# Between two layers of a streamed network: another order of weight chunks on TensorE, and low halves moved from GpSimd to VectorE

## The chip, the cores and the metric

The kernel runs on one core of a Trainium2 chip. The metric is the device time of one execution in microseconds (us). The engines are called TensorE (PE in the profile), VectorE (DVE), ScalarE (ACT), GpSimd (POOL) and SyncE (SP, which here only issues transfers).

## The reference

A sequence of 256 rows of 1024 numbers goes through a first block (a mixer, a cross attention, a mixture of experts, a final norm) and then through two layers of a second block. What matters here is the seam between layer 0 and layer 1 of that second block:

```python
def _rms_norm(x, g):
    xf = x.astype(jnp.float32)
    y = xf * lax.rsqrt(jnp.mean(xf * xf, axis=-1, keepdims=True) + NORM_EPS)
    return (y * g.astype(jnp.float32)).astype(x.dtype)

for i in range(DEPTH_2):                      # two layers
    h = _rms_norm(x, norm_mix_pre[i])
    proj = h @ w_in[i]                        # its first columns here: v and g_out
    ...
    y = (jax.nn.gelu(a, approximate=False) * b) @ ffn_w_down[i]
    x = x + _rms_norm(y, norm_ffn_post[i])    # the seam: the next layer starts with this x
```

## The kernel before

**Chunks of weights.** All weights are streamed from memory in units of 1 MB into a ring of seven slots (`RING`); one unit is two chunks of 128 x 1024. Products are made in three passes, for which every operand is split into a high and a low half: ScalarE writes the high half of a chunk (`WH<-RING`, `hi_half`), then VectorE or GpSimd subtracts it from the chunk and writes the low half (`RINGL<-RING,WH`, `lo_half`). Chunks listed in `LOW_ON_POOL` get their low half on GpSimd, all others on VectorE. There are six buffers for high halves (`NH = 6`): the high half of chunk c waits until TensorE has used up chunk c - 6.

**Chunks of the seam.** Layer l begins with the chunks v0 to v3 (values) and g0 to g3 (output gate), then the pool chunks. The 256 rows of the sequence are two tiles of 128, t = 0 and 1. `stream_tile(c0, j, t)` multiplies chunk j of a group of four into tile t alone: six matmuls of 128x512 (two slices k of the contraction, three passes each). `stream_rows` does the same chunk for both tiles, twelve matmuls. A chunk counts as used up when its tile 1 is done. v_j and g_j need the slices k = 2j and 2j + 1 of the activation.

**The raw activation.** So that the next layer can begin before the norm of its input is known, its first eight chunks are multiplied with the raw activation times the gain (`rh_mix`, `rl_mix`), and the scale of the norm is put in later. `raw_turn` transposes tile t of X with eight small matmuls (`P<-CONS,X`), in two halves of four; ScalarE turns each half into four high slices (`rh_mix`, `norm_hi`), VectorE into four low slices (`rl_mix`, `norm_lo`). `norm_turn` does it again later with the true scale (`P<-DIAG,X`, result in `HA` and `LA`), for all the chunks from pool on.

**The residual.** The end of layer 0 gives four banks, tile 0 in P4 and P5, tile 1 in P6 and P7. For each tile ScalarE sums the squares (`JNK`), VectorE multiplies by the gain (`YB`), forms the mean, ScalarE the root (`SM<-SM`), and VectorE adds the result to X (`X<-YB,SM,X`, twice 128x512 for each tile). `raw_turn` of tile 1 waits for the two X of tile 1.

Order of work is written out by hand in each engine's program: `tensor_layer` for TensorE, `scalar_layer` for ScalarE, `vector_layer` for VectorE, `gpsimd_layer` for GpSimd. Each engine works through its list in order, and waits on semaphores. `hi_until(end)` and `lo_until(end)` do all high or low halves up to chunk `end` that are not yet done. GpSimd's part for the seam is the `tail` of `gpsimd_layer(0)`, three low halves, and the `low` of `gpsimd_layer(1)`, two more:

```python
    tail = [c for c in sorted(LOW_ON_POOL) if c >= chunk_of(1, "v") and c < chunk_of(1, "g")] if l == 0 else []
    ...
    for c in low:
        if c >= chunk_of(l, "g"):
            lo_half(e, m, s, c)
```

Of the kernel before, what the change touches and what calls it, by code (L numbers as in the profile page):

```python
# [23 lines left out]
GROUPS = 16  # L24
# [129 lines left out]
class Port:  # L154
# [70 lines left out]
    def overflow(self, most):  # L225
# [4 lines left out]
        else:  # L230
            name = str(self.engine.engine).split(".")[-1]
            self.engine.br_cond(self.count < most + 1, f"fits_{name}", f"over_{name}").branch_hint(self.seen)
            with self.engine.bass.body(f"over_{name}", valid_engines=[self.engine.engine]):
# [22 lines left out]

LOW_ON_POOL = {1, 3} | {B2 + l * L_CHUNKS + L_AT[n] + i for l, n, i in
                        ((0, "v", 0), (0, "v", 3), (0, "g", 0), (0, "g", 2),
                         (1, "v", 0), (1, "v", 1), (1, "v", 3), (1, "g", 0), (1, "g", 2),
                         (0, "ffn", 12), (1, "ffn", 12))}  # L260


# [420 lines left out]
def rstd_columns(m, t, base):  # L683
    return (m.SM[:, base + 8 + 4 * t + i:base + 9 + 4 * t + i] for i in range(4))
# [21 lines left out]
def rstd_root(e, m, s, tag, t, base=200):  # L706

    rstd_log(e, m, s, tag, t, base)
    rstd_exp(e, m, s, tag, t, base)
# [14 lines left out]
def rstd_end(e, m, s, tag, t, base=200):  # L724

    rstd_step(e, m, s, tag, t, base)
    rstd_last(e, m, s, tag, t, base)
# [11 lines left out]
def norm_turn(e, m, s, tag, x, t):  # L739

    e.wait_ge(*s.diag[tag, t])
    for i in range(2):
        b = 4 + 2 * t + i
        for q in range(4):
            k = 4 * i + q
            for sig, event in m.free[b]:
                e.wait_ge(*sig[event])
            p = e.matmul(m.P[b][:, q * 128:(q + 1) * 128], x[:, t, k * 128:(k + 1) * 128], m.DIAG[:, t, :],
                         start=True, stop=True)
        p.then_inc(*s.turned.up(tag, t, i))  # L750
        m.free[b] = [(s.norm_lo, (tag, t, 4 * i + 3))]


def norm_hi(e, m, s, tag, hi, gain, t, i):

    e.wait_ge(*s.turned[tag, t, i])
    for q in range(4):
        k = 4 * i + q
        e.activation(hi[:, k, t * 128:(t + 1) * 128], m.P[4 + 2 * t + i][:, q * 128:(q + 1) * 128], ACT.Copy,
                     scale=m.par(gain, k)).then_inc(*s.norm_hi.up(tag, t, k))  # L760
# [65 lines left out]
def stream_rows(e, m, s, chunks, j, a, freed, pairs=(0, 1, 2, 3)):  # L826

    end = len(chunks) - 1
    if j == 0:
        for t in range(2):  # L830
            m.next_bank((chunks[0], t), True)
    c = chunks[j]
    hi, lo = m.hi(c), m.lo(c)
    e.wait_ge(*s.hi[c])
    for i in range(2):
        k = 2 * pairs[j] + i
        w = slice(i * 512, (i + 1) * 512)
        for t in range(2):
            b = m.bank[chunks[0], t]
            ta = slice(t * 128, (t + 1) * 128)  # L840
            first, last = j == 0 and i == 0, j == end and i == 1
            sig, event = a.hi_mark(k, t)
            e.wait_ge(*sig[event])
            if first:
                for sig, event in m.free[b]:
                    e.wait_ge(*sig[event])
            e.matmul(m.P[b][:, :], a.hi[:, k, ta], hi[:, w], start=first, stop=False)
            e.wait_ge(*s.lo_of(c)[c])
            e.matmul(m.P[b][:, :], a.hi[:, k, ta], lo[:, w], start=False, stop=False)
            sig, event = a.lo_mark(k, t)  # L850
            e.wait_ge(*sig[event])
            p = e.matmul(m.P[b][:, :], a.lo[:, k, ta], hi[:, w], start=False, stop=last)
            if last and t == 0:
                p.then_inc(*s.stream.up("t0", c))
                m.held.discard(b)
                m.free[b] = [freed(0)]
    p.then_inc(*s.stream.up(c))
    if j == end:
        m.held.discard(b)
        m.free[b] = [freed(1)]  # L860


def stream_tile(e, m, s, c0, j, t, a, freed, pairs=(0, 1, 2, 3)):

    if j == 0:
        m.next_bank((c0, t))
    b = m.bank[c0, t]
    p = rows_part(e, m, s, c0 + j, j, t, b, a, pairs)
    if t == 1:
        p.then_inc(*s.stream.up(c0 + j))  # L870
    elif j == 3:
        p.then_inc(*s.stream.up("t0", c0 + j))
    if j == 3:
        m.free[b] = [freed]
# [1940 lines left out]
def chunk_of(l, name, i=0):  # L2815
    return B2 + l * L_CHUNKS + L_AT[name] + i
# [76 lines left out]
def raw_turn(e, m, s, tag, t, marks):  # L2893

    for i in range(2):
        b = 4 + 2 * t + i
        sig, event = marks[i]
        e.wait_ge(*sig[event])
        for sig, event in m.free[b]:
            e.wait_ge(*sig[event])  # L2900
        for q in range(4):
            k = 4 * i + q
            p = e.transpose(m.P[b][:, q * 128:(q + 1) * 128], m.X[:, t, k * 128:(k + 1) * 128], m.con("ident"))
        p.then_inc(*s.turned.up("raw " + tag, t, i))
        m.free[b] = [(s.norm_lo, ("raw " + tag, t, 4 * i + 3))]
# [12 lines left out]
def tensor_layer(e, m, s, l):  # L2918
    mix, ffn = f"mix{l}", f"ffn{l}"
    chunk = lambda name, i=0: chunk_of(l, name, i)  # L2920
# [1 line left out]
    a = normed(s, mix, m.HA, m.LA)  # L2922


    for t in range(2):
        for j in range(4):
            if (t, j) == (0, 3 if l else 1):
                if l:
                    raw_turn(e, m, s, "mix1", 1, [(s.resid, (0, 1, 1, n)) for n in range(2)])
                else:  # L2930
                    raw_turn(e, m, s, "mix0", 1, [(s.drain, ("moe", GROUPS - 1, 1, n)) for n in range(2)])
            stream_tile(e, m, s, chunk("v"), j, t, raw, (s.evac, ("vv", l, t)))
    step = lambda j: stream_rows(e, m, s, range(chunk("g"), chunk("g") + 4), j, raw, lambda t: (s.evac, ("go", l, t)))
    step(0)
    norm_turn(e, m, s, mix, m.X, 0)
    step(1)
    norm_turn(e, m, s, mix, m.X, 1)
    step(2)
    step(3)
    for i in range(4):  # L2940
        stream_t(e, m, s, chunk("pool", i), a, (s.evac, ("px", l, i)))
    q = lambda h: stream_t(e, m, s, head_chunk(l, 0, h), a, (s.evac, ("q", l, h)))
# [313 lines left out]
def scalar_raw(e, m, s, tag, gain, t):  # L3256
    hi = m.RAW[tag][0]
    norm_hi(e, m, s, "raw " + tag, hi, gain, t, 0)
    norm_hi(e, m, s, "raw " + tag, hi, gain, t, 1)
# [7 lines left out]
def scalar_layer(e, m, s, l):  # L3267
# [202 lines left out]
            hi_until(e, m, s, down_chunk(l, i - 2) + 5)  # L3470
    hi_until(e, m, s, chunk("ffn", 66))
    e.preload_act_table_set("natural_log_exp_and_others")
    e.wait_ge(*s.product["down", l, 0, 0])
    scalar_post(e, m, s, l, 1, 0, 0, m.P[4])
    e.wait_ge(*s.product["down", l, 0, 1])
    scalar_post(e, m, s, l, 1, 0, 1, m.P[5])
    rstd_root(e, m, s, f"post{l}1", 0, base=224)
    if l == 0:
        hi_until(e, m, s, chunk_of(1, "v", 2))
    e.wait_ge(*s.product["down", l, 1, 0])  # L3480
    scalar_post(e, m, s, l, 1, 1, 0, m.P[6])
    e.wait_ge(*s.stream[down_chunk(l, 21)])
    scalar_post(e, m, s, l, 1, 1, 1, m.P[7])
    if l == 0:
        scalar_raw(e, m, s, "mix1", "mix_pre1", 0)
        hi_until(e, m, s, chunk_of(1, "g"))
    rstd_root(e, m, s, f"post{l}1", 1, base=224)


def scalar_beside(e, m, s, l, n):  # L3490
# [67 lines left out]
def scalar_post(e, m, s, l, w, t, n, bank):  # L3558
    square(e, m, s, bank[:, :], m.SM[:, 224 + 2 * t + n:225 + 2 * t + n], (1.0 / D) ** 0.5, f"post{l}{w}", t, n)
# [83 lines left out]
def vector_raw(e, m, s, tag, gain, t):  # L3643
    hi, lo = m.RAW[tag]
    norm_lo(e, m, s, "raw " + tag, hi, lo, gain, t, 0)
    norm_lo(e, m, s, "raw " + tag, hi, lo, gain, t, 1)
# [7 lines left out]
def vector_post(e, m, s, l, w, t, n, bank):  # L3654

    e.wait_ge(*s.square[f"post{l}{w}", t, n])
    e.wait_ge(*s.vec["gain", l, w])
    e.tensor_tensor(m.YB[:, t, n * 512:(n + 1) * 512], bank[:, :], m.GB[:, n * 512:(n + 1) * 512],
                    ALU.mult).then_inc(*s.drain.up("post", l, w, t, n))


def vector_post_tile(e, m, s, l, w, t, bank):

    tag = f"post{l}{w}"
    e.wait_ge(*s.square[tag, t, 1])
    rstd_mean(e, m, s, tag, t, base=224)
    vector_post(e, m, s, l, w, t, 1, bank)
    rstd_end(e, m, s, tag, t, base=224)
    mean, y, a, r = rstd_columns(m, t, 224)
    e.wait_ge(*s.rstd[tag, t])  # L3670
    for n in range(2):
        x = m.X[:, t, n * 512:(n + 1) * 512]
        e.wait_ge(*s.drain["post", l, w, t, n])
        e.scalar_tensor_tensor(x, m.YB[:, t, n * 512:(n + 1) * 512], r, x, ALU.mult, ALU.add).then_inc(*s.resid.up(l, w, t, n))
# [7 lines left out]
def vector_layer(e, m, s, l):  # L3682
# [124 lines left out]
    for i in range(22):  # L3807
# [21 lines left out]
        if 1 < i < 20:  # L3829
            lo_until(e, m, s, down_chunk(l, i - 2) + 5)  # L3830
    lo_until(e, m, s, chunk("ffn", 66))
    vector_post(e, m, s, l, 1, 0, 0, m.P[4])
    vector_post_tile(e, m, s, l, 1, 0, m.P[5])
    if l == 0:
        lo_until(e, m, s, chunk_of(1, "v", 2))
    vector_post(e, m, s, l, 1, 1, 0, m.P[6])
    if l == 0:
        vector_raw(e, m, s, "mix1", "mix_pre1", 0)
        lo_until(e, m, s, chunk_of(1, "g"))
    vector_post_tile(e, m, s, l, 1, 1, m.P[7])  # L3840


def vector_final_norm(e, m, s):
# [362 lines left out]
```

## Time and profile before

| | |
|---|---|
| median of three runs | 1645.8 us (1643.89 to 1646.1) |
| the profiled execution | 1644.13 us, its span 1642.3 us |
| TensorE busy | 1592.4 us, 97% |
| VectorE busy | 937.3 us, 57% |
| ScalarE busy | 729.3 us, 44% |
| GpSimd busy | 90.2 us, 5% |
| mean granted TensorE clock | 0.994 of full |
| transfers | 243 GB/s over the span |

The span runs from the first to the last instruction of the profiled execution. Times inside the trace are us from its start. The seam between the layers lies at 1178 to 1213 us.

### The profile page before, as it was taken

How to read it: one execution, taken by the hardware profiler on the slowest of the kernel's cores; microseconds unless marked ns; L12 is line 12 of the kernel's file. 1: busy time of each engine (PE TensorE's matmuls, PEld its weight loads, DVE VectorE, ACT ScalarE, POOL GpSimd, SP SyncE). 2: the span in 40 equal slices, each digit the busy share in tenths (PEclk: the TensorE clock that was granted, in tenths of full speed). 3: DMA queues.
4: the chain of work that ended last, by engine and by line, in shares of the span. 5: the costliest groups of instructions: out<-in, count | busy, mean ns of one | idle time of the engine just before them, and what ended most of it. 6: DMA issues, size and time to landing. Idle time of an engine off the chain costs nothing.

```text
span 1642.3 us, 22882 instructions
## 1 busy us (share of the span) xinstructions
PE 1592.4 (97%) x9321; PEld 1200.3 (73%) x9321; DVE 937.3 (57%) x1595; ACT 729.3 (44%) x1385; POOL 90.2 (5%) x81
## 2 busy tenths in 40 slices
PE   7999999999999999989999999999899999999998
PEld 6987885444333434339997889999799978889997
DVE  5967655232332332247675567766767855677665
ACT  6755542110110111047663357555566633575554
POOL 1010000000000000014001000000230010000000
PEclk9999999999999999999999999999999999999999
DMA  9433578999999999994444445555443444545550
GB/s 358 179 129 132 195 292 314 389 378 423 424 424 400 424 423 424 423 377 178 143 169 155 175 171 189 180 182 187 154 177 132 180 154 166 180 167 183 190 192 27
DMA packets 57414, 399.83 MB, mean 243 GB/s; under 512 B 6612, under 2 KB 7029, under 8 KB 9946
## 3 DMA queue, kind: packets, MB, share of 16 engines
q1 hardware_dynamic: 57306, 398.34, 63.0%
q8 instruction: 74, 1.21, 0.3%
q14 instruction: 34, 0.28, 0.0%
HBM read 397.26 MB, written 1.05 MB: 243 GB/s over the span
## 4 chain that ended last, share of the span: by engine, by line
PE 82%; DMA 12%; DVE 3%; ACT 2%; POOL 0%; issue 0%; SPq 0%; DVEq 0%; POOLq 0%
PE P L171 80%; DMA RING<-in_ws_dram 8%; PE P L174 2%; DMA ew<-in_ws_dram 1%; DMA W<-in_hw_dram 1%; DMA ez<-in_ws_dram 1%; DVE RINGL L183 1%; DVE X L189 0%; POOL GV L183 0%; ACT WH L177 0%; DVE SM L189 0%; DVE rl_mix L189 0%; ACT JNK L177 0%; DVE YB L183 0%; SPq L216 0%
## 5 line engine op out<-in xcount | busy, mean ns | idle before, releaser
L183 DVE TENSOR_TENSOR RINGL<-RING,WH 128x1024 fp32r<-128x1024 f32 x338 | 418.9, 1272 | 130.2 <-ACT WH L177 129.0
L177 ACT ACTIVATE WH<-RING 128x1024 fp32r<-128x1024 f32 x351 | 358.1, 1055 | 53.0 <-PE P L171 50.8
L171 PE MATMUL P<-HA,WH 128*128 128x256 f32 x1208 | 345.3, 286 | 0.0
L171 PE MATMUL P<-LA,WH 128*128 128x256 f32 x1208 | 340.5, 282 | 0.0
L171 PE MATMUL P<-HA,RINGL 128*128 128x256 f32 x1208 | 340.5, 282 | 0.0
L171 PEld LDWEIGHTS P<-HA,WH 128*128 128x128 f32 x1208 | 227.9, 189 | 5.8 <-issue 3.0
L171 PEld LDWEIGHTS P<-HA,RINGL 128*128 128x128 f32 x1208 | 228.4, 189 | 2.1
L171 PEld LDWEIGHTS P<-LA,WH 128*128 128x128 f32 x1208 | 228.8, 189 | 0.0
L171 PE MATMUL P<-RING,XT 128*64 128x512 f32 x632 | 143.9, 595 | 8.2 <-DMA RING<-in_ws_dram 8.1
L171 PEld LDWEIGHTS P<-RING,XT 128*64 128x64 f32 x632 | 44.1, 137 | 103.4 <-issue 78.2
L171 PE MATMUL P<-WH,HA 128*128 128x512 f32 x272 | 110.5, 406 | 1.3 <-ACT VN L177 1.3
L183 DVE TENSOR_TENSOR GS<-P,GS 128x512 f32<-128x512 f32 x16 | 11.1, 692 | 173.1 <-PE P L171 173.1
L171 PE MATMUL P<-RINGL,HA 128*128 128x512 f32 x272 | 107.4, 395 | 1.8 <-POOL RINGL L183 1.8
L171 PE MATMUL P<-WH,LA 128*128 128x512 f32 x272 | 106.9, 393 | 0.0
L189 DVE SCALAR_TENSOR_TENSOR YSL<-P,SM,YSH 128x512 fp32r<-128x512 f32 x32 | 22.6, 747 | 127.2 <-ACT YSH L177 127.2
L177 ACT ACTIVATE YSH<-P,SM 128x512 fp32r<-128x512 f32 x32 | 20.3, 684 | 142.1 <-PE P L171 142.1
L177 ACT ACTIVATE HT<-P 128x512 f32<-128x512 f32 x16 | 9.6, 598 | 153.7 <-PE P L174 153.7
L189 DVE SCALAR_TENSOR_TENSOR CVT<-QPC,PARS,CVT 128x256 f32<-128x256 f32 x104 | 53.5, 515 | 36.4 <-ACT CVT L177 34.2
L171 PE MATMUL P<-WH,FL 128*128 128x512 f32 x176 | 69.8, 397 | 0.0
L171 PE MATMUL P<-RINGL,FH 128*128 128x512 f32 x176 | 69.4, 395 | 0.0
L171 PE MATMUL P<-WH,FH 128*128 128x512 f32 x176 | 69.3, 394 | 0.0
L177 ACT ACTIVATE QPC<-P 128x256 f32<-128x256 f32 x68 | 26.0, 382 | 86.2 <-PE P L171 86.2
(404 smaller groups left out, 2676.8 us busy)
## 6 DMA issues: line engine op xcount, KB each, us to landing
RING<-in_ws_dram SPq DMA_DIRECT2D x288, 1024.0 KB, 5.0
ew<-in_ws_dram SPq DMA_DIRECT2D x47, 1024.0 KB, 21.5
ez<-in_ws_dram SPq DMA_DIRECT2D x16, 1024.0 KB, 20.0
ek<-in_ws_dram SPq DMA_DIRECT2D x6, 1024.0 KB, 10.9
ef<-in_ws_dram SPq DMA_DIRECT2D x4, 1024.0 KB, 10.7
eha<-in_ws_dram SPq DMA_DIRECT2D x2, 1024.0 KB, 5.1
ela<-in_ws_dram SPq DMA_DIRECT2D x2, 1024.0 KB, 6.8
TAB<-in_dft_dram SPq DMA_DIRECT2D x2, 1024.0 KB, 5.6
```

The lines of the kernel that those rows point to most:

```text
L171: return self.engine.matmul(*a, **k) if self.engine else self
L174: return self.engine.transpose(*a) if self.engine else self
L177: return self.engine.activation(*a, **k) if self.engine else self
L183: return self.engine.tensor_tensor(*a) if self.engine else self
L189: return self.engine.scalar_tensor_tensor(*a) if self.engine else self
```

## The change

The change touches the seam between layer 0 and layer 1 only. It has three parts. The chunks v0, v1, v3, g0 and g2 of layer 1 get their low half on VectorE, no longer on GpSimd. On ScalarE and VectorE the halves of the first chunks move ahead: v0 to v2 (ScalarE) and v0, v1 (VectorE) come before the squares and gains of the last product, and the residual sum of tile 1 (`vector_post_sum`) comes after the low halves of v3 and g0. On TensorE tile 0 goes through v0 to v3 and g0 before the raw turn of tile 1, and through g1 right behind it; then tile 1 does the same six chunks. g2 and g3 stay with the norm turns, now tile by tile.

```diff
--- before.py
+++ after.py
@@ -256,7 +256,6 @@
 
 LOW_ON_POOL = {1, 3} | {B2 + l * L_CHUNKS + L_AT[n] + i for l, n, i in
                         ((0, "v", 0), (0, "v", 3), (0, "g", 0), (0, "g", 2),
-                         (1, "v", 0), (1, "v", 1), (1, "v", 3), (1, "g", 0), (1, "g", 2),
                          (0, "ffn", 12), (1, "ffn", 12))}
 
 
@@ -2922,21 +2921,38 @@
     a = normed(s, mix, m.HA, m.LA)
 
 
-    for t in range(2):
+    v = lambda j, t: stream_tile(e, m, s, chunk("v"), j, t, raw, (s.evac, ("vv", l, t)))
+    go = lambda j, t: stream_tile(e, m, s, chunk("g"), j, t, raw, (s.evac, ("go", l, t)))
+    if l == 0:
+        for t in range(2):
+            for j in range(4):
+                if (t, j) == (0, 1):
+                    raw_turn(e, m, s, "mix0", 1, [(s.drain, ("moe", GROUPS - 1, 1, n)) for n in range(2)])
+                v(j, t)
+        step = lambda j: stream_rows(e, m, s, range(chunk("g"), chunk("g") + 4), j, raw, lambda t: (s.evac, ("go", l, t)))
+        step(0)
+        norm_turn(e, m, s, mix, m.X, 0)
+        step(1)
+        norm_turn(e, m, s, mix, m.X, 1)
+        step(2)
+        step(3)
+    else:
+
         for j in range(4):
-            if (t, j) == (0, 3 if l else 1):
-                if l:
-                    raw_turn(e, m, s, "mix1", 1, [(s.resid, (0, 1, 1, n)) for n in range(2)])
-                else:
-                    raw_turn(e, m, s, "mix0", 1, [(s.drain, ("moe", GROUPS - 1, 1, n)) for n in range(2)])
-            stream_tile(e, m, s, chunk("v"), j, t, raw, (s.evac, ("vv", l, t)))
-    step = lambda j: stream_rows(e, m, s, range(chunk("g"), chunk("g") + 4), j, raw, lambda t: (s.evac, ("go", l, t)))
-    step(0)
-    norm_turn(e, m, s, mix, m.X, 0)
-    step(1)
-    norm_turn(e, m, s, mix, m.X, 1)
-    step(2)
-    step(3)
+            v(j, 0)
+        go(0, 0)
+        raw_turn(e, m, s, "mix1", 1, [(s.resid, (0, 1, 1, n)) for n in range(2)])
+        go(1, 0)
+        for j in range(4):
+            v(j, 1)
+        go(0, 1)
+        go(1, 1)
+        norm_turn(e, m, s, mix, m.X, 0)
+        go(2, 0)
+        go(2, 1)
+        norm_turn(e, m, s, mix, m.X, 1)
+        go(3, 0)
+        go(3, 1)
     for i in range(4):
         stream_t(e, m, s, chunk("pool", i), a, (s.evac, ("px", l, i)))
     q = lambda h: stream_t(e, m, s, head_chunk(l, 0, h), a, (s.evac, ("q", l, h)))
@@ -3470,21 +3486,25 @@
             hi_until(e, m, s, down_chunk(l, i - 2) + 5)
     hi_until(e, m, s, chunk("ffn", 66))
     e.preload_act_table_set("natural_log_exp_and_others")
+    if l == 0:
+        hi_until(e, m, s, chunk_of(1, "v", 3))
     e.wait_ge(*s.product["down", l, 0, 0])
     scalar_post(e, m, s, l, 1, 0, 0, m.P[4])
     e.wait_ge(*s.product["down", l, 0, 1])
     scalar_post(e, m, s, l, 1, 0, 1, m.P[5])
     rstd_root(e, m, s, f"post{l}1", 0, base=224)
     if l == 0:
-        hi_until(e, m, s, chunk_of(1, "v", 2))
+        hi_until(e, m, s, chunk_of(1, "g"))
     e.wait_ge(*s.product["down", l, 1, 0])
     scalar_post(e, m, s, l, 1, 1, 0, m.P[6])
     e.wait_ge(*s.stream[down_chunk(l, 21)])
     scalar_post(e, m, s, l, 1, 1, 1, m.P[7])
+    hi = m.RAW["mix1"][0]
     if l == 0:
-        scalar_raw(e, m, s, "mix1", "mix_pre1", 0)
-        hi_until(e, m, s, chunk_of(1, "g"))
+        norm_hi(e, m, s, "raw mix1", hi, "mix_pre1", 0, 0)
     rstd_root(e, m, s, f"post{l}1", 1, base=224)
+    if l == 0:
+        norm_hi(e, m, s, "raw mix1", hi, "mix_pre1", 0, 1)
 
 
 def scalar_beside(e, m, s, l, n):
@@ -3661,13 +3681,21 @@
 
 def vector_post_tile(e, m, s, l, w, t, bank):
 
+    vector_post_end(e, m, s, l, w, t, bank)
+    vector_post_sum(e, m, s, l, w, t)
+
+
+def vector_post_end(e, m, s, l, w, t, bank):
     tag = f"post{l}{w}"
     e.wait_ge(*s.square[tag, t, 1])
     rstd_mean(e, m, s, tag, t, base=224)
     vector_post(e, m, s, l, w, t, 1, bank)
     rstd_end(e, m, s, tag, t, base=224)
+
+
+def vector_post_sum(e, m, s, l, w, t):
     mean, y, a, r = rstd_columns(m, t, 224)
-    e.wait_ge(*s.rstd[tag, t])
+    e.wait_ge(*s.rstd[f"post{l}{w}", t])
     for n in range(2):
         x = m.X[:, t, n * 512:(n + 1) * 512]
         e.wait_ge(*s.drain["post", l, w, t, n])
@@ -3829,15 +3857,21 @@
         if 1 < i < 20:
             lo_until(e, m, s, down_chunk(l, i - 2) + 5)
     lo_until(e, m, s, chunk("ffn", 66))
+    if l == 0:
+        lo_until(e, m, s, chunk_of(1, "v", 2))
     vector_post(e, m, s, l, 1, 0, 0, m.P[4])
     vector_post_tile(e, m, s, l, 1, 0, m.P[5])
     if l == 0:
-        lo_until(e, m, s, chunk_of(1, "v", 2))
+        lo_until(e, m, s, chunk_of(1, "v", 3))
     vector_post(e, m, s, l, 1, 1, 0, m.P[6])
+    hi, lo = m.RAW["mix1"]
     if l == 0:
-        vector_raw(e, m, s, "mix1", "mix_pre1", 0)
-        lo_until(e, m, s, chunk_of(1, "g"))
-    vector_post_tile(e, m, s, l, 1, 1, m.P[7])
+        norm_lo(e, m, s, "raw mix1", hi, lo, "mix_pre1", 0, 0)
+    vector_post_end(e, m, s, l, 1, 1, m.P[7])
+    if l == 0:
+        norm_lo(e, m, s, "raw mix1", hi, lo, "mix_pre1", 0, 1)
+        lo_until(e, m, s, chunk_of(1, "g", 1))
+    vector_post_sum(e, m, s, l, 1, 1)
 
 
 def vector_final_norm(e, m, s):
```

On VectorE, at the seam, before the change (the rows from the sum of tile 0 into X; `rl_mix` are the low slices of the raw activation, `RINGL` low halves of weights, `SM` the small columns of the norm):

```order
L189 SCALAR_TENSOR_TENSOR X<-YB,SM,X 128x512 x2
L183 TENSOR_TENSOR YB<-P,GB 128x512
L189 SCALAR_TENSOR_TENSOR rl_mix_188<-P,PARS,rh_mix_187 128x128 x8
L183 TENSOR_TENSOR RINGL<-RING,WH 128x1024
L186 TENSOR_SCALAR SM<-SM 128x1
L183 TENSOR_TENSOR YB<-P,GB 128x512
L189 SCALAR_TENSOR_TENSOR SM<-SM 128x1 x2
L189 SCALAR_TENSOR_TENSOR X<-YB,SM,X 128x512 x2
L183 TENSOR_TENSOR RINGL<-RING,WH 128x1024
```

The same place of VectorE with the change:

```order
L189 SCALAR_TENSOR_TENSOR X<-YB,SM,X 128x512 x2
L183 TENSOR_TENSOR RINGL<-RING,WH 128x1024
L183 TENSOR_TENSOR YB<-P,GB 128x512
L189 SCALAR_TENSOR_TENSOR rl_mix_188<-P,PARS,rh_mix_187 128x128 x4
L186 TENSOR_SCALAR SM<-SM 128x1
L183 TENSOR_TENSOR YB<-P,GB 128x512
L189 SCALAR_TENSOR_TENSOR SM<-SM 128x1 x2
L189 SCALAR_TENSOR_TENSOR rl_mix_188<-P,PARS,rh_mix_187 128x128 x4
L183 TENSOR_TENSOR RINGL<-RING,WH 128x1024 x2
L189 SCALAR_TENSOR_TENSOR X<-YB,SM,X 128x512 x2
L183 TENSOR_TENSOR RINGL<-RING,WH 128x1024
```

Between the two sums into X there is now one low half ahead of the gain (v2) and two behind the low slices (v3, g0), where there was one (v2); the norm's small steps moved between the two halves of the low slices.

On ScalarE, at the seam, before the change (`JNK` are the squares, `SM` the roots, `WH` high halves of weights, `rh_mix` high slices of the raw activation):

```order
L180 ACT_TABLE_LOAD
L177 ACTIVATE JNK,SM<-P 128x512 x2
L177 ACTIVATE SM<-SM 128x1 x2
L177 ACTIVATE WH<-RING 128x1024 x2
L177 ACTIVATE JNK,SM<-P 128x512 x2
L177 ACTIVATE rh_mix_187<-P,PARS 128x128 x8
L177 ACTIVATE WH<-RING 128x1024 x2
L177 ACTIVATE SM<-SM 128x1 x2
L177 ACTIVATE WH<-RING 128x1024 x2
```

The same place of ScalarE with the change:

```order
L180 ACT_TABLE_LOAD
L177 ACTIVATE WH<-RING 128x1024 x3
L177 ACTIVATE JNK,SM<-P 128x512 x2
L177 ACTIVATE SM<-SM 128x1 x2
L177 ACTIVATE WH<-RING 128x1024
L177 ACTIVATE JNK,SM<-P 128x512 x2
L177 ACTIVATE rh_mix_187<-P,PARS 128x128 x4
L177 ACTIVATE SM<-SM 128x1 x2
L177 ACTIVATE rh_mix_187<-P,PARS 128x128 x4
L177 ACTIVATE WH<-RING 128x1024 x2
```

Three high halves now stand ahead of the first squares, and the roots of tile 1 between the two halves of the high slices.

## Rows read from the trace of the kernel before

**Rows 1.** Page, part 1: engine, busy us, share of the span, instructions.

```profile
PE 1592.4 (97%) x9321; PEld 1200.3 (73%) x9321; DVE 937.3 (57%) x1595; ACT 729.3 (44%) x1385; POOL 90.2 (5%) x81
```

**Rows 2.** TensorE's waits, 1176 to 1642 us: in total, times, longest.

```profile
PE P L174 <- DVE X L189: 4.4, 3, 1.8
PE P L171 <- DVE RINGL L183: 0.3, 1, 0.3
```

**Rows 3.** Timeline of TensorE: start, us, engine, line, out<-in, count [idle before].

```profile
1177.95 0.60 PE L174 MATMUL P<-CONS,X 128*128 128x128 f32 x4
1179.48 0.66 PE L174 MATMUL P<-CONS,X 128*128 128x128 f32 x4 [0.93 <-DVE X L189]
...
1181.37 0.40 PE L171 MATMUL P<-WH,rh_mix 128*128 128x512 f32 x1
...
1182.99 0.40 PE L171 MATMUL P<-WH,rh_mix 128*128 128x512 f32 x1
1183.66 0.50 PE L171 MATMUL P<-RINGL,rh_mix 128*128 128x512 f32 x1 [0.27 <-DVE RINGL L183]
...
1184.69 0.39 PE L171 MATMUL P<-WH,rl_mix 128*128 128x512 f32 x1
1186.91 1.11 PE L174 MATMUL P<-CONS,X 128*128 128x128 f32 x4 [1.83 <-DVE X L189]
1189.66 1.12 PE L174 MATMUL P<-CONS,X 128*128 128x128 f32 x4 [1.64 <-DVE X L189]
1190.43 0.78 PE L171 MATMUL P<-WH,rh_mix 128*128 128x512 f32 x1
...
1193.82 0.40 PE L171 MATMUL P<-WH,rl_mix 128*128 128x512 f32 x1
...
1201.61 1.95 PE L171 MATMUL P<-DIAG,X 128*128 128x128 f32 x16
...
1213.42 0.28 PE L171 MATMUL P<-HA,WH 128*128 128x256 f32 x1
```

**Rows 4.** Timeline of VectorE between the layers.

```profile
1174.01 0.69 DVE L183 TENSOR_TENSOR YB<-P,GB 128x512 f32<-128x512 f32 x1 [3.81 <-ACT JNK L177]
...
1175.88 3.55 DVE L189 SCALAR_TENSOR_TENSOR X<-YB,SM,X 128x512 f32<-128x512 f32 x2
...
1179.95 1.11 DVE L189 SCALAR_TENSOR_TENSOR rl_mix<-P,PARS,rh_mix 128x128 fp32r<-128x128 f32 x4
...
1182.40 1.21 DVE L183 TENSOR_TENSOR RINGL<-RING,WH 128x1024 fp32r<-128x1024 f32 x1
...
1186.10 3.50 DVE L189 SCALAR_TENSOR_TENSOR X<-YB,SM,X 128x512 f32<-128x512 f32 x2
```

**Rows 5.** Timeline of GpSimd between the layers.

```profile
1176.42 5.26 POOL L183 TENSOR_TENSOR RINGL<-RING,WH 128x1024 fp32r<-128x1024 f32 x2 [153.25 <-ACT WH L177]
...
1186.18 2.87 POOL L183 TENSOR_TENSOR RINGL<-RING,WH 128x1024 fp32r<-128x1024 f32 x1
```

**Rows 6.** Timeline of VectorE, end of layer 1, where GpSimd is idle.

```profile
1634.22 1.41 DVE L189 SCALAR_TENSOR_TENSOR X<-YB,SM,X 128x512 f32<-128x512 f32 x2
```

**Rows 7.** Timeline of ScalarE between the layers.

```profile
1168.96 1.28 ACT L180 ACT_TABLE_LOAD   x1
...
1178.74 1.14 ACT L177 ACTIVATE rh_mix<-P,PARS 128x128 fp32r<-128x128 f32 x4
...
1183.77 0.44 ACT L177 ACTIVATE SM<-SM 128x1 f32<-128x1 f32 x2 [0.56 <-DVE SM L186]
```

**Rows 8.** Windows: us, busy of each engine, granted clock, DMA share, GB/s.

```profile
508.00:516.00 8.00, 8.00 (x24) 2.39 (x26) 0.53 (x1) 0.00 (x0) 0.00 (x0) 0.60 1.01 424
723.00:729.00 6.00, 3.55 (x18) 2.29 (x18) 5.45 (x11) 6.00 (x14) 3.38 (x2) 1.00 1.01 422
1176.00:1190.00 14.00, 9.33 (x42) 6.38 (x41) 13.64 (x19) 10.18 (x24) 11.03 (x7) 0.88 0.35 120
1186.80:1193.50 6.70, 4.95 (x15) 3.95 (x16) 6.32 (x12) 3.83 (x13) 2.25 (x1) 0.50 0.00 0
```

## The prediction

> **What bounds the kernel now.** The page's first part says that TensorE is busy for 1592.4 of 1642.3 us, while VectorE and ScalarE are at 57% and 44% [rows 1]: only what TensorE loses can be won. The view of TensorE's waits from the end of layer 0 to the end of the program shows where that is. There are four waits in all, 4.7 us together: three for a sum into X ahead of transposes, one for a low half [rows 2]. The last of them is at 1189.66 [rows 3]; in the 450 us of layer 1 behind it TensorE waits for nothing. A microsecond that TensorE gains at the seam therefore stays gained, as long as the engines that feed it move up as well, and everything on them there hangs on TensorE's progress or on the same X.
>
> The timeline of TensorE through the seam [rows 3] gives the pace. From 1193.82 to 1201.61 it issues 34 matmuls of 128x512 without a gap: 7.79 / 34 = 0.229 us each, so one chunk for one tile (six matmuls) is 1.37 us. Against that pace the seam loses time at four places behind 1181.37, where the second chunk begins:
> - at v2 (1182.99 to 1183.66 where one step of 0.23 would do): 0.44 us, for its low half; v1 waits similarly for about 0.1;
> - from 1184.92 (1184.69 + 0.23) to 1186.91: 1.99 us, for the first X of tile 1;
> - in the raw turn of tile 1: it begins at 1186.91 and the next matmul stands at 1190.43, 3.52 us. The turn of tile 0 gives four transposes in 0.60; four more at that pace bring a turn to about 1.05. Lost: 2.47 us, the wait for the second X (1.64) and a slow clock;
> - from 1190.43 to 1193.82 eight matmuls take 3.39 instead of 1.83 us: 1.56 lost. The windows show why: the granted clock is 0.50 of full, the 1.2 GHz level, in 1186.8 to 1193.5, right behind the idle time of 1.83 us [rows 8].
>
> That is 0.54 + 1.99 + 2.47 + 1.56 = 6.6 us in which TensorE stands or crawls, and it is the most that a change of the seam can win behind 1181.37.
>
> **Why X is late.** VectorE's two sums into X of tile 1 take 3.50 us, and those of tile 0 take 3.55 [rows 4]. The same two instructions at the end of layer 1 take 1.41 [rows 6]. The difference is what runs on GpSimd: its low halves occupy 1176.42 to 1181.68 and 1186.18 to 1189.05 [rows 5], and each pair of sums lies across the beginning of one. VectorE's own low half, 1.21 us, and its low slices out of PSUM, 1.11 us for four [rows 4], have the length that they have elsewhere.
>
> **The change part by part.**
>
> *GpSimd.* Five low halves leave it. Each returns as one VectorE instruction of 1.21 us (about 1.15 from start to start). The two pairs of sums fall from 3.5 to 1.41, a gain of 2.1 us each.
>
> *v0 and v1 early.* VectorE is idle for 3.81 us before 1174.01 [rows 4], so both low halves, 2.4 us, lie in a hole and cost nothing; without the hole they would delay the gain by 2.4 us. On ScalarE three high halves of about 1.0 us stand behind the table load, which ends at 1170.24 (1168.96 + 1.28 [rows 7]). The third needs a buffer that TensorE frees at about 1172.4, so it ends at 1173.6 and the first squares start about 0.3 us late. VectorE absorbs that: the sum of tile 0 ends at 1177.6 instead of 1179.4.
>
> *Raw turn of tile 0.* It no longer waits in its middle (the 0.93 of 1179.48 [rows 3]). That gives nothing by itself: ScalarE starts its high slices at 1178.74 [rows 7], behind its squares, VectorE starts the low slices at 1179.95 as before, and TensorE's third matmul of v0 needs the first of them. So 1181.37 stays where it is, and I count from there.
>
> *Walk behind 1181.37.* TensorE does v1 until 1182.7. On VectorE the first four low slices end at 1181.1; mean, gain and small steps follow, with ScalarE's roots at 1181.3 to 1181.7 (it started 0.24 behind the mean before too, 1183.77 [rows 7]). Then come ScalarE's second four high slices, to 1182.8, and VectorE's low ones, 1182.8 to 1183.9. v2 needs the first of these at 1183.2: just in time; it ends at 1184.1. v3 needs its low half, which VectorE makes behind the slices, 1183.9 to 1185.1. TensorE waits 0.75 us here: this is the new wait, and the only one of any size. v3 ends at 1186.25, g0, whose low half is ready at 1186.2, at 1187.6. The sums of tile 1 follow at 1186.15 and end at 1187.55, so the turn at 1187.6 finds both. It ends at 1188.7, just when the low half of g1 is ready (1188.7). g1 ends at 1190.1. By then the slices of tile 1 have begun (ScalarE from about 1188.35, VectorE from 1189.5), and the next six chunks run at full pace for 8.25 us, to 1198.3.
>
> *Norm turns and behind.* At 1198.3 the first norm turn starts; before it started at 1201.61 [rows 3] with two chunk tiles less done. Its scale is ready at about 1195. Two norm turns (1.95 busy [rows 3], of which the next matmuls cover 0.25, so 1.70 each) and the four tiles of g2 and g3 (5.5 us) put the first pool chunk at about 1207.4, against 1213.42 [rows 3]. g2's low half on VectorE ends near 1197.7 and is needed at 1200: hidden, as is g0's extra 1.15 in the walk. The six high buffers hold exactly v0 to g1; g2's needs v0's, which tile 1 frees at 1191.5. SyncE's fetches hang on the same marks and come slightly earlier.
>
> **The sum.** The losses of 6.6 us, less the new wait of 0.75 (0.8 with small ones): 5.8 us. The walk gives 6.0. I take 5.9. The profiled execution took 1644.13 us (span 1642.3 and 1.8 around it); it would take 1638.2. It lies 1.7 under the median of 1645.8, so the median goes to **1639.9**, a change of 0.36%. About 0.2% (3.3 us) is what a measurement of this kernel can tell from no change.
>
> **A rule that speaks against it.** VectorE is busy for 13.64 of the 14 us from 1176 to 1190 [rows 8], and the change gives it more to do there. The Trainium skill, Perfetto Trace Analysis, section Optimizing Scalar/DVE Operations, says that when VectorE is saturated, handing work to ScalarE or even GpSimd may make sense, and adds that the two share a read port, so that it might not help between them. Going by its first half the change would win next to nothing, as the second rival works out; by its second half, the sum above. The rows lean to the second half: the pairs of sums lose 2.1 us each beside GpSimd.
>
> **The rivals.**
> 1. *The clock falls anyway.* The forecast has TensorE idle for 0.6 us at 1179.7 and 0.75 at 1184.4. Against a fall: at the first layer's seam it was busy for only 3.55 of 6 us and the clock stayed at 1.00 (723 to 729 [rows 8]). For it: at this seam it fell. A half rate stretch of 6.7 us like the one before, now under full load, costs 3.35, and the gain is 2.5: 1643.3. Chance 13%.
> 2. *VectorE becomes the bound.* If GpSimd was not what stretched the sums, they keep 3.5 us, and with two more halves (2.3 us) ahead of them the second X comes at 1189.6 + 2.3 = 1191.9. Behind it lie a piece of the turn, g1 and ten more tiles (15.1 us) and two norm turns: pool at 1210.9, and with the clock fallen by 1.6 more at 1212.5. Gain about 1: 1644.9. Rows 6 speak against it. Chance 7%.
> 3. *Half way.* One wait more of 1 to 2.5 us, for instance the pair of sums not wholly freed, or a high half late behind the roots: gain 4, 1641.8. Chance 10%.
> 4. *Slower.* One mechanism: the clock falls at 1184.4 and stays low under full load. Each microsecond at the 1.2 GHz level costs half of one, so the gain is gone at 11.8 us of it, and at 19 us the kernel is 3.6 us slower: 1649.4. The stretch around 508 to 516 shows 0.60 over 8 us, about 6.4 us at the low level [rows 8], and the one of this seam 6.7; neither is near. Chance 4%.
>
> **How the numbers follow.** Forecast 66%, rivals 13, 7, 10 and 4%. The forecast has its own spread of about 1.5 us (all 6.6 won, or a wait of 1.5 more, and the spread of medians): 1637.8 to 1641.6. To leave out no more than 2 in 10 the range goes up to rival 1: 1637.5 to 1643.6. Faster by over 0.2% (under 1642.5): nearly all of the forecast, two thirds of rival 3, a fourth of rival 1, together 0.75. Slower: 0.04. The rest is 0.21.
>
> **What the changed profile would show.** Right: no GpSimd low halves at the seam; pairs of sums at 1.4 us; one TensorE wait for RINGL of about 0.75 at v3 and none for X; clock 1.00 through 1178 to 1213; from 1181.4 to the first pool chunk 26 us instead of 32.05; no waits behind it. Wrong would be sums still at 3.5, a clock of 0.50 somewhere behind 1179, a wait of over a microsecond at v2 or at the first norm turn, or TensorE waiting in layer 1 where it did not before.

## The result

| | before | changed |
|---|---|---|
| median of six runs | 1644.08 us (1642.81 to 1646.1) | 1637.42 us (1636.43 to 1637.92) |
| profiled execution | 1644.13 us, span 1642.3 | 1636.43 us, span 1634.6 |
| the seam (see below) | 46.70 us | 40.47 us |

The ratio is 0.9962, with a 95% interval of 0.9953 to 0.9972: 6.2 us faster (4.6 to 7.7), where 5.9 were forecast. The median of the kernel before came out at 1644.08 over six runs, 1.7 us under the 1645.8 of three runs that the forecast started from. So the absolute number, 1637.42, lies 2.5 us under the forecast 1639.9 and just under the low end of its range (1637.5), most of it by that starting level and not by the change.

The first rows of the page of the changed kernel answer to [rows 1]: GpSimd is busy for 14 us less, TensorE for 4.9 us less. Of these 4.9 us, 2.7 are the slow clock at the seam, as the windows below show; the rest had arisen ahead of it, where the two programs are the same.

```profile
span 1634.6 us, 22882 instructions
...
PE 1587.5 (97%) x9321; PEld 1197.4 (73%) x9321; DVE 937.0 (57%) x1600; ACT 729.0 (45%) x1385; POOL 76.1 (5%) x76
```

TensorE's waits from the end of layer 0 to the end of the program answer to [rows 2]. The three waits for a sum into X are gone; 1.1 us are left, and none lies behind the seam.

```profile
PE P L171 <- DVE RINGL L183: 0.5, 1, 0.5
PE P L171 <- DVE rl_mix L189: 0.4, 1, 0.4
PE P L171 <- issue: 0.2, 1, 0.2
```

The timeline of TensorE through the seam answers to [rows 3]:

```profile
1165.26 0.28 PE L171 MATMUL P<-LA,WH 128*128 128x256 f32 x1
...
1178.85 0.50 PE L171 MATMUL P<-WH,rl_mix 128*128 128x512 f32 x1 [0.41 <-DVE rl_mix L189]
...
1179.87 0.39 PE L171 MATMUL P<-WH,rh_mix 128*128 128x512 f32 x1
...
1182.66 0.40 PE L171 MATMUL P<-WH,rh_mix 128*128 128x512 f32 x1
1183.54 0.50 PE L171 MATMUL P<-RINGL,rh_mix 128*128 128x512 f32 x1 [0.48 <-DVE RINGL L183]
...
1186.17 1.04 PE L174 MATMUL P<-CONS,X 128*128 128x128 f32 x8
1186.96 0.47 PE L171 MATMUL P<-WH,rh_mix 128*128 128x512 f32 x1
...
1196.66 1.95 PE L171 MATMUL P<-DIAG,X 128*128 128x128 f32 x16
...
1205.73 0.28 PE L171 MATMUL P<-HA,WH 128*128 128x256 f32 x1
```

"The seam" is from here on the time from the last matmul of the last up chunk (`P<-LA,WH`, at 1165.26 here, at 1166.72 before) to the first of the first pool chunk (1205.73 here, 1213.42 before). It is a better measure of a change of this size than one execution's span: the spans differ by 7.7 us, of which 1.46 had arisen before this stretch, where the two programs are the same. Behind it both take 428.9 us. The windows of exactly this stretch, in the kernel before and in the changed one (us, then busy time of TensorE, of its weight loads, of VectorE, ScalarE and GpSimd, then granted clock, DMA share, GB/s):

```profile
1166.72:1213.42 46.70, 42.03 (x196) 33.79 (x194) 32.37 (x65) 30.44 (x74) 13.43 (x8) 0.93 0.40 144
```

```profile
1165.26:1205.73 40.47, 39.37 (x196) 32.21 (x195) 30.00 (x70) 30.05 (x74) 0.50 (x3) 1.00 0.50 182
```

The same 196 matmuls are busy for 2.66 us less, and TensorE is idle for 1.10 us instead of 4.67: 6.23 together.

The timeline of VectorE answers to [rows 4], and the windows to [rows 8]:

```profile
1169.88 2.36 DVE L183 TENSOR_TENSOR RINGL<-RING,WH 128x1024 fp32r<-128x1024 f32 x2 [1.15 <-ACT WH L177]
1172.80 0.69 DVE L183 TENSOR_TENSOR YB<-P,GB 128x512 f32<-128x512 f32 x1 [0.56 <-ACT JNK L177]
...
1174.57 1.42 DVE L189 SCALAR_TENSOR_TENSOR X<-YB,SM,X 128x512 f32<-128x512 f32 x2
1175.90 1.22 DVE L183 TENSOR_TENSOR RINGL<-RING,WH 128x1024 fp32r<-128x1024 f32 x1
...
1178.44 1.13 DVE L189 SCALAR_TENSOR_TENSOR rl_mix<-P,PARS,rh_mix 128x128 fp32r<-128x128 f32 x4 [0.72 <-ACT rh_mix L177]
...
1181.22 1.13 DVE L189 SCALAR_TENSOR_TENSOR rl_mix<-P,PARS,rh_mix 128x128 fp32r<-128x128 f32 x4 [0.62 <-ACT rh_mix L177]
1182.27 2.35 DVE L183 TENSOR_TENSOR RINGL<-RING,WH 128x1024 fp32r<-128x1024 f32 x2
1184.54 1.41 DVE L189 SCALAR_TENSOR_TENSOR X<-YB,SM,X 128x512 f32<-128x512 f32 x2
```

```profile
1176.00:1190.00 14.00, 12.90 (x62) 9.93 (x61) 11.72 (x27) 8.93 (x28) 0.00 (x0) 1.00 0.28 102
1190.00:1205.00 15.00, 15.00 (x83) 12.96 (x82) 9.98 (x29) 11.90 (x33) 0.00 (x0) 1.00 0.74 268
```

Both pairs of sums take 1.4 us. Two low halves fill the hole behind 1169.9. The clock is at 1.00 throughout. VectorE, which has more instructions than before, is busy for 11.72 of these 14 us instead of 13.64.

### The profile page after: what moved, and what is told of

Same layout as the page of the kernel before. It is cut to its first block, busy times and chain, and to the rows that moved or that the text cites. A ratio compares the mean times of both kernels' runs of the same rounds, so it can differ in the third digit from the quotient of the medians.

```text
span 1634.6 us, 22882 instructions
## 1 busy us (share of the span) xinstructions
PE 1587.5 (97%) x9321; PEld 1197.4 (73%) x9321; DVE 937.0 (57%) x1600; ACT 729.0 (45%) x1385; POOL 76.1 (5%) x76
## 3 DMA queue, kind: packets, MB, share of 16 engines
q8 instruction: 74, 1.21, 0.3%
HBM read 397.26 MB, written 1.05 MB: 244 GB/s over the span
## 4 chain that ended last, share of the span: by engine, by line
PE 82%; DMA 13%; DVE 3%; ACT 2%; issue 0%; SPq 0%; DVEq 0%
PE P L171 80%; DMA RING<-in_ws_dram 8%; DMA ew<-in_ws_dram 2%; PE P L174 2%; DMA ez<-in_ws_dram 1%; DMA W<-in_hw_dram 1%; DVE RINGL L183 1%; ACT WH L177 0%; DVE rl_mix L189 0%; ACT JNK L177 0%; DVE SM L189 0%; ACT SM L177 0%; ACT L180 0%; DVE HS L189 0%; ACT rh_mix L177 0%
## 5 line engine op out<-in xcount | busy, mean ns | idle before, releaser
L183 DVE TENSOR_TENSOR RINGL<-RING,WH 128x1024 fp32r<-128x1024 f32 x343 | 424.4, 1270 | 128.0 <-ACT WH L177 127.0
```

The source lines that it names most:

```text
L183: return self.engine.tensor_tensor(*a) if self.engine else self
```

## The experiments

Each kernel was compared with runs of the kernel before on the same chip (medians 1644.1, 1644.2 and 1644.05 us, and a single run of 1644.55). The seam is read from each run's own profile. "Run-ahead" is TensorE's new order (tile 0 goes on through v3 and g0 before the raw turn of tile 1, and through g1 behind it), "early split" the new order of ScalarE and VectorE (the halves of the first chunks ahead of the squares, gains and sums).

| kernel | median us | ratio, interval | seam us |
|---|---|---|---|
| before (three executions profiled) | | | 46.70, 46.13, 47.49 |
| changed (two) | 1637.4 | 0.9962 (0.9953 to 0.9972) | 40.47, 40.48 |
| GpSimd part alone | 1639.6 | 0.9975 (0.9964 to 0.9987) | 42.55 |
| changed, low halves kept on GpSimd | 1638.1 | 0.9966 (0.9954 to 0.9978) | 42.78 |
| changed, TensorE's old order | 1641.1 | 0.9984 (0.9975 to 0.9993) | 44.29 |
| changed, without the early split | 1638.8 | 0.9967 (0.9953 to 0.9980) | 42.28 |
| changed, g2 alone on GpSimd | 1638.2 | 0.9962 (0.9947 to 0.9977) | 40.47 |
| layer 0's seam off GpSimd too | 1636.4 | 0.9951 (0.9937 to 0.9964) | 40.50 |
| the same, v3's low half earlier | 1635.0 | 0.9945 (0.9931 to 0.9959) | 40.15 |
| the same, low slices first at layer 0 | 1635.4 | 0.9947 (0.9933 to 0.9960) | 40.14 |

**The GpSimd part alone.** The kernel before, with

```diff
-                         (1, "v", 0), (1, "v", 1), (1, "v", 3), (1, "g", 0), (1, "g", 2),
```

> The kernel before with one part of the change: the five chunks of layer 1 get their low half on VectorE; every order stays. Theory (GpSimd's low halves stretch the sums into X, and the new order hides the halves that come back): the sums of tile 1 take 1.4 us instead of 3.5, but v0, v1 and v3 now stand ahead of them on VectorE (3.5 us), so the first one ends only about 2 us earlier and the first matmuls of v0 start late; gain 2 to 4 us of the 6.2. Rival A (the neighbourhood of GpSimd is all there is to it): gain about 6 us. Rival B (the order is all): no gain, or slower by up to 1 us.

Measured: 4.1 us by the ratio, 4.15 by the seam, just above the 2 to 4 us that were expected. VectorE's timeline shows four low halves between the sums, and both pairs at 1.4 us. TensorE's shows what is left: one wait for the first sum of tile 1, and then a whole turn in one piece.

```profile
1175.18 1.41 DVE L189 SCALAR_TENSOR_TENSOR X<-YB,SM,X 128x512 f32<-128x512 f32 x2
1176.52 2.35 DVE L183 TENSOR_TENSOR RINGL<-RING,WH 128x1024 fp32r<-128x1024 f32 x2
...
1181.46 2.34 DVE L183 TENSOR_TENSOR RINGL<-RING,WH 128x1024 fp32r<-128x1024 f32 x2
...
1184.88 1.42 DVE L189 SCALAR_TENSOR_TENSOR X<-YB,SM,X 128x512 f32<-128x512 f32 x2
```

```profile
1185.68 1.32 PE L174 MATMUL P<-CONS,X 128*128 128x128 f32 x8 [1.54 <-DVE X L189]
1186.76 0.48 PE L171 MATMUL P<-WH,rh_mix 128*128 128x512 f32 x1
```

**The new orders, with GpSimd kept.** The changed kernel with that line put back.

> The changed kernel with the five low halves put back on GpSimd; the new orders stay. Theory: VectorE has 5.8 us less to do but its sums meet GpSimd again: the pair of tile 0 meets v3's low half and ends near 3 us, everything behind it is about 1 us late, g0's low half (2.5 us on GpSimd) lands about 1.5 us late and meets the sums of tile 1. Loss 1 to 2.5 us against the changed kernel, so a gain of 4 to 5 against before. Rival (VectorE, 94% busy before at the seam, is the bound and the move to it costs): as fast as the changed kernel or up to 1 us faster.

The seam is 2.3 us longer than in the changed kernel although VectorE has five instructions less, and 3.9 shorter than before. VectorE's timeline shows why: both pairs of sums are back at over 3.5 us, each beside one low half of GpSimd.

```profile
1174.34 3.53 DVE L189 SCALAR_TENSOR_TENSOR X<-YB,SM,X 128x512 f32<-128x512 f32 x2
...
1183.34 3.58 DVE L189 SCALAR_TENSOR_TENSOR X<-YB,SM,X 128x512 f32<-128x512 f32 x2
```

```profile
1174.50 2.82 POOL L183 TENSOR_TENSOR RINGL<-RING,WH 128x1024 fp32r<-128x1024 f32 x1 [0.41 <-ACT WH L177]
...
1183.28 2.41 POOL L183 TENSOR_TENSOR RINGL<-RING,WH 128x1024 fp32r<-128x1024 f32 x1 [5.59 <-ACT WH L177]
```

TensorE waits 1.45 us in the middle of the first turn (0.93 in the kernel before) and 0.87 for the first low slice, which comes 1.7 us later than in the changed kernel (1179.92 is 4.05 behind the turn's start, 1178.85 was 2.36). The clock falls there: seven matmuls from 1179.92 to 1183.05 take 3.13 us instead of 1.7. That makes 3.1 us; 0.8 come back, 0.65 of them because v3's low half, made by GpSimd, is no longer waited for.

```profile
1177.93 0.66 PE L174 MATMUL P<-CONS,X 128*128 128x128 f32 x4 [1.45 <-DVE X L189]
...
1179.92 0.80 PE L171 MATMUL P<-WH,rl_mix 128*128 128x512 f32 x1 [0.87 <-DVE rl_mix L189]
...
1183.05 0.40 PE L171 MATMUL P<-WH,rh_mix 128*128 128x512 f32 x1
```

The medians show less of it (5.6 us gained, 3.6 to 7.6 by the interval) than the seams; they cannot tell 1638.1 from 1637.4.

**TensorE's old order.** In the changed kernel `tensor_layer` is as before:

```diff
-        for j in range(4):
-            v(j, 0)
-        go(0, 0)
-        raw_turn(e, m, s, "mix1", 1, ...)
...
+    for t in range(2):
+        for j in range(4):
+            if (t, j) == (0, 3 if l else 1):
+                if l:
+                    raw_turn(e, m, s, "mix1", 1, ...)
...
```

> The changed kernel with TensorE's order of before at the seam (raw turn of tile 1 behind v2, g0 to g3 for both tiles at once). Theory: the second sum of tile 1 still ends near 1185.9, but TensorE is done with v2 at 1182.7 and idles 2.5 us; behind that the clock falls to half for a while, as before. Two tiles of chunks (2.75 us) less cover, minus the 0.5 wait at v3: a loss of 2.2 us by the idle time and 1.6 more by the clock, gain against before about 2.4 us (4.0 if the clock stays up). Rival (the order on TensorE is worth nothing, only VectorE's sums count): gain 6.2 us as with the whole change.

The wait is 2.51 us, the clock falls behind it, and the seam is 2.41 us shorter than before: as the theory had it. It is also 1.74 us longer than with the GpSimd part alone, and the rows say why. Counted from the start of the seam, the early split brings TensorE to v2's end 0.5 us sooner (17.6 instead of 18.1 us), but as it also puts the low half of g0 ahead of the sums, they begin 0.4 us later (19.3 instead of 18.85). The wait is 0.97 us longer, and nothing is won. And the clock, which stayed up behind 1.54 us, fell: eight matmuls from 1187.53 to 1191.02 take 3.49 us instead of 1.83.

```profile
1186.45 1.35 PE L174 MATMUL P<-CONS,X 128*128 128x128 f32 x8 [2.51 <-DVE X L189]
1187.53 0.71 PE L171 MATMUL P<-WH,rh_mix 128*128 128x512 f32 x1
1188.03 0.63 PE L171 MATMUL P<-RINGL,rh_mix 128*128 128x512 f32 x1
...
1191.02 0.40 PE L171 MATMUL P<-WH,rl_mix 128*128 128x512 f32 x1
```

**Without the early split.** Two parts of the change, TensorE's order and the GpSimd part; ScalarE and VectorE keep their order of before.

> TensorE's new order and no low halves on GpSimd, but ScalarE's and VectorE's orders of before: the change without its early split. Theory: the three parts need each other. VectorE makes g0's low half only behind the sums, so TensorE, done with v3 on tile 0, waits about 1.8 us for it where the kernel with the GpSimd part alone waited 1.5 for the sum: the run-ahead wins nothing by itself, seam about 42.5 us (46.7 before, 42.55 with the GpSimd part alone, 40.5 with all), gain against before about 4 us. Rival (the run-ahead is worth its 2.4 us in any case): seam 40.5, gain 6 us.

The seam is 42.28 us. The wait moved from the sum to g0's low half (1.59 us idle), as expected, and the run-ahead by itself gives 0.3 us over the GpSimd part alone, where run-ahead and early split together give 2.1.

```profile
1188.21 0.50 PE L171 MATMUL P<-RINGL,rh_mix 128*128 128x512 f32 x1 [1.59 <-DVE RINGL L183]
```

**g2 alone on GpSimd.** One chunk put back into `LOW_ON_POOL`: `(1, "g", 2)`.

> The changed kernel with g2's low half alone back on GpSimd, at about 1195, where no sum into X lies and TensorE is four tiles away. Theory (it is the place that costs, not the use of GpSimd): the seam stays at 40.5 us, the time within 1 us of the changed kernel; VectorE's low half of g3 beside it may take 2.5 us and delay nothing. Rival (each low half on GpSimd costs): 1 to 2 us slower.

The seam is 40.47, to a hundredth that of the changed kernel. VectorE's two low halves beside it take 3.71 us instead of 2.35, and nobody waits for them.

```profile
1197.15 2.39 POOL L183 TENSOR_TENSOR RINGL<-RING,WH 128x1024 fp32r<-128x1024 f32 x1 [27.24 <-ACT WH L177]
```

```profile
1198.05 3.71 DVE L183 TENSOR_TENSOR RINGL<-RING,WH 128x1024 fp32r<-128x1024 f32 x2 [2.71 <-ACT WH L177]
```

**Layer 0's seam too.** On top of the change:

```diff
-                        ((0, "v", 0), (0, "v", 3), (0, "g", 0), (0, "g", 2),
-                         (0, "ffn", 12), (1, "ffn", 12))}
+                        ((0, "ffn", 12), (1, "ffn", 12))}
...
 def gpsimd_between(e, m, s):
-    lo_half(e, m, s, B2)
-    lo_half(e, m, s, B2 + 3)
+    pass
```

> The changed kernel with the seam ahead of layer 0 treated like it in one respect: v0, v3, g0 and g2 of layer 0 also get their low half on VectorE, with no change of order. Theory (each low half of VectorE beside one of GpSimd takes 2.5 instead of 1.2 us at 723 to 735): VectorE wins 1.3 us for each of three such meetings and pays 1.15 for each of three halves, so the result is within 1 us of the changed kernel, either way; the rows to look at are TensorE's waits at 724 to 736 (3.2 us before). Rival: with GpSimd silent it is over 1.5 us faster.

The stretch from the first raw matmul of layer 0 to its first pool chunk took 30.73 us in the changed kernel and 30.74 in the one before; here it takes 29.99, and in the next run, whose program is the same there, 28.87. The difference between those two is the clock, as shown at the end. TensorE's waits of 0.68 (for GpSimd), 0.41 and 0.36 us are gone; the one for a low slice (1.45 us in the changed kernel) is left, at 1.50. The theory expected at most 1 us, the rival over 1.5; the stretch is 0.7 us shorter with a fall of the clock and 1.9 without, so each is right of one execution. The median is 1.0 us lower, which its interval does not tell from either.

**v3's low half earlier.** On top of that:

```diff
+        lo_until(e, m, s, chunk_of(1, "g"))
         norm_lo(e, m, s, "raw mix1", hi, lo, "mix_pre1", 0, 1)
         lo_until(e, m, s, chunk_of(1, "g", 1))
```

> The kernel with both layers' seams off GpSimd, and v3's low half put ahead of the second four low slices, into the 0.6 us in which VectorE waits for ScalarE. Theory (the 0.65 us that the changed kernel loses at v3 is a queue on VectorE): the wait for v3's low half goes, v2 waits 0.3 us for its slices in its place; seam 40.2 instead of 40.5, too little for the median. Rival (the slices are tighter than I think): a wait of 0.6 or more at v2, seam 40.5 to 40.9.

As expected: the wait at v3 is gone, v2 waits 0.20 (0.35 from its pace) for its slices, the seam is 40.15. This kernel has the lowest median, 9.1 us under before, 0.55%; the intervals do not tell it from the kernels of the runs around it.

```profile
1179.98 0.50 PE L171 MATMUL P<-WH,rl_mix 128*128 128x512 f32 x1 [0.20 <-DVE rl_mix L189]
```

**Slices first at layer 0.** On top of that, in `vector_between`:

```diff
+    hi, lo = m.RAW["mix0"]
-    lo_until(e, m, s, B2 + 2)
+    lo_until(e, m, s, B2 + 1)
     vector_combine_part(e, m, s, g, 1, 1)
-    vector_raw(e, m, s, "mix0", "gfin", 0)
+    norm_lo(e, m, s, "raw mix0", hi, lo, "gfin", 0, 0)
+    lo_until(e, m, s, B2 + 2)
+    norm_lo(e, m, s, "raw mix0", hi, lo, "gfin", 0, 1)
```

> As the run before it, and ahead of layer 0 VectorE makes v1's low half between the two halves of the low slices of tile 0, not ahead of them. Theory: the first low slice is ready 1.1 us earlier, TensorE's wait of 1.50 us for it shrinks to about 0.4, no other grows by more than 0.3; about 0.8 us less than the run before it. Rival (v1's low half is then late itself, or the first wait is for ScalarE's high slices): no difference.

A miss. The wait shrinks from 1.50 to 0.35 us as foreseen, but two others appear, 0.40 for a low half and 0.43 for a slice, and the stretch is 28.82 us against 28.87. There VectorE is the bound, busy for 13.8 of the first 14.2 us in both kernels: an order only chooses where TensorE waits for it.

```profile
722.96 0.50 PE L171 MATMUL P<-WH,rl_mix 128*128 128x512 f32 x1 [0.35 <-DVE rl_mix L189]
...
727.04 0.50 PE L171 MATMUL P<-RINGL,rh_mix 128*128 128x512 f32 x1 [0.40 <-DVE RINGL L183]
...
730.71 0.50 PE L171 MATMUL P<-WH,rl_mix 128*128 128x512 f32 x1 [0.43 <-DVE rl_mix L189]
```

**Once more, for the clock.** The kernel before and the changed one, unchanged.

> The kernel before, unchanged, profiled once more: does the clock fall at the seam in every execution? Theory (my sum counts 1.56 us of matmuls at the low clock as part of what the change wins): it falls again behind the 1.8 us of idle time, seam 46.7 us. Rival (a fall behind a gap of this size is chance): the clock stays at 1.00, seam 44.5 to 45, and the time is some 2 us lower.

> The same once more, for a third execution of the kernel before: theory 46.7 us for the seam, rival 44.5 to 45.

> The changed kernel, profiled once more: with no gap over 0.5 us at the seam the clock stays at 1.00 there and the seam is 40.5 us again; if a fall is chance even here, it is 41.5 to 44.

The seam of before is 46.13 and 47.49 us, besides 46.70; the changed kernel's is 40.48. In all executions of before the clock falls at the waits for the sums, as the theory had it, but not at the same place nor for the same time: in the first, the first four transposes behind the wait of 1.83 us are already slow (1.11 us); in the second and third these take 0.66 us, and the next four, behind a gap of 2.10, take 1.11 and 1.12. So windows over about the same stretch show different shares, first in the second execution, then in the third (the granted clock is the third number from the end):

```profile
1186.80:1193.50 6.70, 5.13 (x19) 4.34 (x20) 5.24 (x12) 4.44 (x18) 0.96 (x1) 0.75 0.01 2
```

```profile
1186.00:1194.00 8.00, 4.37 (x15) 3.56 (x16) 7.63 (x14) 4.42 (x14) 3.68 (x5) 0.70 0.01 2
1189.50:1195.50 6.00, 5.22 (x15) 4.25 (x16) 4.46 (x12) 3.88 (x15) 0.18 (x1) 0.50 0.01 3
```

## Why the prediction was right

*What bounds the kernel.* Right. The seam is shorter by TensorE's idle time (3.57 us) and its slow time (2.66 us), and in the 430 us behind it no wait appeared.

*GpSimd and the sums.* Shown from both sides: 1.4 us without GpSimd, with the old order and with the new; 3.5 with it, in both. The prediction missed one more instruction of this kind. A third low half of GpSimd, v3's, met the two steps of one column each that stand right before the second sums, and they took 1.82 us in the kernel before instead of 0.40 in the changed one, 1.4 us more on the way to the X that TensorE waited for:

```profile
1183.29 2.57 POOL L183 TENSOR_TENSOR RINGL<-RING,WH 128x1024 fp32r<-128x1024 f32 x1 [1.61 <-ACT WH L177]
```

```profile
1184.25 1.82 DVE L189 SCALAR_TENSOR_TENSOR SM<-SM 128x1 f32<-128x1 f32 x2
```

The prediction also noted that VectorE's own low half, 1.21 us, has its usual length. That one stands at 1182.40, where GpSimd is idle (1181.68 to 1183.29) for most of it; beside GpSimd low halves stretch too (3.71 us for two in the run with g2 on GpSimd).

The first half of the rule that was weighed in the prediction (VectorE saturated, so hand work to GpSimd) would have been a mistake at this place: handing it back cost 2.3 us of seam in its one profile, 1.4 of them by the clock behind the longer waits. Its second half agrees with the trace. The Trainium skill, SBUF - State Buffer, section Who interferes with whom, says that a VectorE instruction with two SBUF inputs contends with a GpSimd instruction that reads SBUF. The trace agrees: the sums have X and YB as inputs, and beside a GpSimd low half of 2.4 to 2.8 us a pair takes 2.1 us more.

*Early halves.* Right: they lie in the hole. The first squares of the changed kernel stand at 1172.10; moved by the 1.46 us by which the whole stretch is early, that is 0.27 later than before (0.3 forecast).

*The raw turn of tile 0.* Right: v1 starts at 1179.87, or 1181.33 on the clock of before, where it started at 1181.37.

*The walk.* v3's wait is the one new wait, 0.48 idle or 0.65 from the pace of matmuls (0.75 forecast); the 0.21 and 0.41 us at v0 stand in the place of the 0.93 in the middle of the first turn. The turn of tile 1 takes 0.79 us, not 1.05. From v1 to the first pool chunk it is 25.86 us (26 forecast, 32.05 before). The walk's last terms were added up 0.2 too high: 1198.3, two norm turns of 1.70 and 5.5 make 1207.2, not 1207.4, which brings the walk to the 6.2 that were measured.

*The sum.* 5.8 by the losses, 6.0 by the walk, 6.23 by the seam of the two profiles. The term that was not as firm as it looked is the clock's: I took 1.56 us as a constant of the kernel before. Its other executions show that it varies, so that the seam's gain is 5.7 to 7.0 us, depending on which execution of before is taken. By the three profiles of before (mean 46.77) and the two of the changed kernel it is 6.3.

*The parts.* What the prediction did not work out is that the parts do not add up. GpSimd's part alone shortens the seam by 4.15 us; with the early split added it is 2.41 (4.1 without the clock's 1.66), with the run-ahead added 4.42, with both 6.23. The two orders with GpSimd's halves kept give 3.92, so the GpSimd part is worth 4.15 on the old orders and 2.31 on the new. Run-ahead without the split waits for g0's low half, the split without run-ahead waits for the sum: each puts the wait where the other would have had work. These are differences of single profiles. By the intervals of the ratios every kernel of the table is faster than before, and the one with TensorE's old order is slower than the whole change; the rest they do not tell apart.

*The rivals.* The clock did not fall at this seam in the two profiles of the changed kernel, whose longest gap there is 0.5 us. The row that the prediction set against a fall (1.00 from 723 to 729, at layer 0's seam) was luck of one execution: the clock falls there in the second and third profile of the same kernel. At this seam no gap of the 0.6 and 0.75 us that were forecast came about, so whether the clock holds behind such gaps is not shown. VectorE as the bound, with sums that keep 3.5 us, is refuted for this seam; at layer 0's it is the bound.

## What to carry to other kernels

When a busy VectorE shares a critical stretch with GpSimd, look at the lengths of its instructions with two SBUF inputs and compare them with the same ones elsewhere; if they stretch and TensorE waits for what hangs on them, taking work back from GpSimd can free more time than it costs. Where nobody waits for VectorE a low half on GpSimd costs nothing, though it stretches the ones beside it too. An order of use (run-ahead on TensorE) and an order of supply (which half is made first) belong together; with GpSimd out of the way each alone was worth 0.3 us or less here, both together 2.1. Where the engine that feeds is the bound, reordering only moves the wait.

## What was not expected of the hardware

Whether the clock falls behind a gap of about 1.5 us is not fixed by the program. The plainest case is one kernel profiled twice. At layer 0's seam the changed kernel has the same wait of 1.45 us for a slice in both profiles; behind it the clock stayed up in the first and fell in the second. Of the three profiles of the kernel before it stayed up in one and fell in two. In all, among ten profiles with the same program there, it fell in seven. Windows behind that wait in the first and the second profile of the changed kernel:

```profile
726.00:730.00 4.00, 3.63 (x19) 2.77 (x19) 4.00 (x9) 4.00 (x11) 3.50 (x5) 1.00 1.01 421
```

```profile
726.00:730.00 4.00, 3.77 (x14) 3.23 (x15) 4.00 (x9) 3.67 (x8) 3.24 (x5) 0.57 1.01 417
```

Without GpSimd there, two kernels with the same program at layer 0's seam had the same wait of 1.50 us for a slice (starting at 726.38 and 724.98); behind it one got the 1.2 GHz level for about 3.4 us and the other none, and the stretch took 29.99 and 28.87 us. Windows of the first and of the second:

```profile
727.00:730.00 3.00, 3.00 (x12) 2.59 (x11) 3.00 (x7) 3.00 (x6) 0.00 (x0) 0.50 1.02 425
```

```profile
725.50:729.00 3.50, 3.50 (x21) 2.95 (x21) 3.50 (x8) 3.50 (x7) 0.00 (x0) 1.00 1.01 417
```

At the seam between the layers it fell in all three executions of before, among gaps of 1.8 and 1.6 to 2.1 us, behind one of 2.51, and behind 1.45 followed by 0.87; it did not behind single ones of 1.54 and 1.59. And a fall costs next to nothing where TensorE is not the bound: at layer 0's seam with GpSimd at work the stretch is 30.72 to 30.74 us in the three profiles without a fall and 30.71 to 30.83 in the seven with one.
